# Banded attention of a two-block layer, two heads at a time, with its weights divided ahead of their transposes

## What is computed

```
logits = einsum('bhrnqd,bhrnkd->bhrnqk', qb, kb) * Dh ** -0.5 + bias
p = exp(logits - m); s = sum(p); o = einsum('bhrnqk,bhrnkd->bhrnqd', p, v) / s
A = einsum('bhncd,bhnjd->bhncj', q_in, k_in) * tril
U = einsum('bhnjd,bhnjv->bhndv', k_end, vc)
return intra + inter            # A v + q_in S_prev
```

## Time and profile before

| | |
|---|---|
| median of three runs | 2418.72 us |
| the profiled execution's own time | 2418.39 us |
| its span | 2416.7 us, at a granted clock of 0.998 |
| TensorE busy | 2396.2 us (99%) |
| VectorE, ScalarE, GpSimd busy | 1427.8 (59%), 1189.1 (49%), 216.1 us (9%) |
| moved by DMA | 430.74 MB, mean 178 GB/s |
| chain that ended last | TensorE 97%, VectorE 1%, ScalarE 1% |

### The profile page before, as it was taken

How to read it: one execution, slowest core, us unless ns; L and a number is a source line. 1 busy time by engine, 2 the same in 40 slices (tenths; PEclk the granted TensorE clock), 3 DMA queues, 4 the chain that set the end, 5 groups by cost and what they waited for, 6 DMA issues and landing times.

```text
span 2416.7 us, 28770 instructions
## 1 busy us (share of the span) xinstructions
PE 2396.2 (99%) x11618; PEld 1966.8 (81%) x11618; DVE 1427.8 (59%) x1709; ACT 1189.1 (49%) x1645; POOL 216.1 (9%) x324
## 2 busy tenths in 40 slices
PE   9999999999999999999999999999999999999998
PEld 7888888888888888888887778778888888888886
DVE  5655665565566545665855455567555555556775
ACT  6544554454455445555655344456444444446564
POOL 0052004206200420000000000000000000000000
PEclk9999999999999999999999999999999999999999
DMA  6555455455445555666665444346665555555554
GB/s 207 194 168 162 151 180 175 157 174 157 158 157 174 187 157 179 226 201 200 217 200 185 146 142 140 118 161 202 206 197 184 190 190 191 192 191 192 192 192 139
DMA packets 235970, 430.74 MB, mean 178 GB/s; under 512 B 27492, under 2 KB 30445, under 8 KB 235838
## 3 DMA queue, kind: packets, MB, share of 16 engines
q1 hardware_dynamic: 222848, 413.30, 52.2%
q10 hardware_dynamic: 12990, 15.60, 2.2%
HBM read 423.59 MB, written 5.28 MB: 177 GB/s over the span
## 4 chain that ended last, share of the span: by engine, by line
PE 97%; DVE 1%; ACT 1%; issue 0%; POOL 0%; ACTq 0%; POOLq 0%; DVEq 0%
PE gemm L1323 29%; PE gemm L1325 29%; PE gemm L1324 29%; PE side L889 3%; PE side L1258 1%; PE side L1279 1%; PE side L994 1%; PE side L1244 1%; PE side L899 0%; DVE arena L1744 0%; PE side L1215 0%; PE side L1114 0%; PE side L1060 0%; PE side L998 0%; PE side L962 0%
## 5 line engine op out<-in xcount | busy, mean ns | idle before, releaser
L1738 DVE TENSOR_TENSOR weight_lo<-weight_raw,weight_hi 128x1024 fp32r<-128x1024 f32 x780 | 965.0, 1240 | 762.1 <-ACT weight_hi L1351 761.2
L1351 ACT ACTIVATE weight_hi<-weight_raw 128x1024 fp32r<-128x1024 f32 x780 | 822.1, 1056 | 854.2 <-PE gemm L1325 834.8
L1323 PE MATMUL gemm<-weight_hi,x_hi 128*128 128x512 f32 x2368 | 943.1, 398 | 3.7 <-DVE x_lo L1744 2.1
L1325 PE MATMUL gemm<-weight_hi,x_lo 128*128 128x512 f32 x2368 | 923.5, 390 | 0.0
L1324 PE MATMUL gemm<-weight_lo,x_hi 128*128 128x512 f32 x2368 | 921.9, 389 | 0.0
L1323 PEld LDWEIGHTS gemm<-weight_hi,x_hi 128*128 128x128 f32 x2368 | 444.9, 188 | 102.9 <-issue 12.8
L1325 PEld LDWEIGHTS gemm<-weight_hi,x_lo 128*128 128x128 f32 x2368 | 444.5, 188 | 94.9
L1324 PEld LDWEIGHTS gemm<-weight_lo,x_hi 128*128 128x128 f32 x2368 | 445.2, 188 | 89.4 <-issue 1.4
L1323 PE MATMUL gemm<-weight_hi,lhs_hi 128*128 128x512 f32 x736 | 288.0, 391 | 0.0
L1325 PE MATMUL gemm<-weight_hi,lhs_lo 128*128 128x512 f32 x736 | 287.1, 390 | 0.0
L1324 PE MATMUL gemm<-weight_lo,lhs_hi 128*128 128x512 f32 x736 | 287.1, 390 | 0.0
(11 more groups left out here) (189 smaller groups left out, 1069.3 us busy)
## 6 DMA issues: line engine op xcount, KB each, us to landing
weight_raw<-in_w_in_dram SPq DMA_DIRECT2D x207, 1024.0 KB, 5.1
weight_raw<-in_w_out_dram SPq DMA_DIRECT2D x48, 1024.0 KB, 5.1
weight_raw<-in_w_gate_dram SPq DMA_DIRECT2D x44, 1024.0 KB, 5.1
weight_raw<-in_w_up_dram SPq DMA_DIRECT2D x44, 1024.0 KB, 5.2
weight_raw<-in_w_down_dram SPq DMA_DIRECT2D x44, 1024.0 KB, 5.0
arena<-rel_line ACTq DMA_DIRECT2D x8, 384.0 KB, 5.1
arena<-in_x_dram SPq DMA_DIRECT2D x4, 512.0 KB, 9.3
arena<-delta_blocks ACTq DMA_DIRECT2D x16, 128.0 KB, 5.2
```

Of the source, the lines that this page charges most:

```text
L1323: e.matmul(pair[i][:, :], xh[:, s], wh, start=first, stop=False)
L1325: m = e.matmul(pair[i][:, :], xl[:, s], wh, start=False, stop=last)
L1351: return e.activation(o, i, ACT.Copy, scale=scale)
L1738: return e.tensor_tensor(o, x, y, op)
```

## The change

- The job gv1 stands ahead of av1: gv1 460, av1 468, gr1 476.
- Attention works on pairs of heads (c = 0 to 3 in a half). `alog` of a pair is four matmuls, alternating between the heads, into two banks; VectorE does 4 adds and one maximum over 1024 columns, ScalarE 4 exponentials. `anorm` is new: VectorE takes 4 reciprocals, and GpSimd multiplies the weights (128x1024) by them. `aturn` is 8 transposes into two banks and two copies to a block of its own (`ET`). `apv` has v stationary (128x64) and the turned weights moving (256 columns); the two heads write partitions 0 to 63 and 64 to 127 of a bank that two pairs share. ScalarE copies it, tokens reversed, straight to `acts`. `aout` and `ao` are gone.
- Slots: `alog` 440, 442, 444, 446 (464 to 470), `anorm` three slots behind each, `aturn` five, `apv` 447, 449, 451, 453 in half 0, and 477, 477, 479, 479 in half 1.
- GLA: `gstate` computes both heads in one slot (four matmuls, four banks), every second slot; `go` computes both heads in one slot, and each head has state blocks of its own. `gsq` stands right behind `go`: ScalarE copies the two banks to SBUF and squares from there into PSUM; `ggated` reads SBUF. Slots of hp 0: `gstate` 422, 424, 426, `go` 428, `gsq` 429, the rest as before. Of hp 1: `gsum` 456, 457, `gscore` 459, `gkend` 460, `gstate` 476, 478, 480, `go` 482, `gsq` 483, `ggated` 485, `gout` 486.
- The last VectorE operation of `ggate2` is a step of its own, `ggate3`, three slots later.

```diff
-    j2("aq1", C_AQ + NC), j2("ak1", C_AK + NC), j2("av1", C_AV + NC)
-    j2("gv1", C_GV + NC), j2("gr1", C_GR + NC)
+    j2("aq1", C_AQ + NC), j2("ak1", C_AK + NC)
+    j2("gv1", C_GV + NC), j2("av1", C_AV + NC), j2("gr1", C_GR + NC)
...
+        for c in range(4):
+            put(s + 4 + 2 * c, "alog", half, c), put(s + 7 + 2 * c, "anorm", half, c)
+            put(s + 9 + 2 * c, "aturn", half, c)
+            put(s + 11 + 2 * c if half == 0 else END["av1"] + 1 + 2 * (c // 2), "apv", half, c)
+    gla_at(put, 1, END["aq1"] + 4, END["aq1"] + 7, END["gv1"] + 8, END["gr1"])
...
+def gla_at(put, hp, s, k, v, t):
...
+    for z in range(3):
+        put(v + 2 * z, "gstate", hp, z)
+    put(v + 6, "go", hp), put(v + 7, "gsq", hp)
...
# TensorE
+        def alog(half, c):
...
+            p = [open_bank("alog", half, c, z) for z in range(2)]
             for i in range(NT):
+                for z in range(2):
+                    rows = slice(z * AT_D, (z + 1) * AT_D)
+                    m = e.matmul(p[z][:, i * T:(i + 1) * T], qT[rows, c * T + i * P:c * T + (i + 1) * P],
+                                 kT[rows, c * T:(c + 1) * T], start=True, stop=True)
...
+        def aturn(half, c):
+            E = blk("E", half, c)
+            w.wait_ge(*at("pool:anorm", half, c))
...
+        def apv(half, c):
...
+            p = open_bank("apv", half, c) if c % 2 == 0 else bank("apv", half, c - 1)
+            for k in range(NT):
+                for z in range(2):
+                    at_ = k * NC + (2 * c + z) * AT_D
+                    m = e.matmul(p[z * AT_D:(z + 1) * AT_D, (c % 2) * T:(c % 2 + 1) * T], v[:, at_:at_ + AT_D],
+                                 ET[:, z * NC + k * T:z * NC + (k + 1) * T], start=k == 0, stop=k == NT - 1)
...
+            for hh in range(2):
+                for d, n in ((0, z), (1, NCH - 1 - z)):
+                    b0 = (n % 2) * GL_C
+                    p = open_bank("gstate", hp, z, hh, d)
...
# ScalarE
+            for g in range(2 * NT):
+                s = e.activation(E[:, g * T:(g + 1) * T], E[:, g * T:(g + 1) * T], ACT.Exp, bias=nm[:, g:g + 1],
+                                 accum_out=sums[:, g:g + 1])
...
# VectorE
+            for z in range(2):
+                for i in range(NT):
+                    s = tt(E[:, z * NC + i * T:z * NC + (i + 1) * T], bank("alog", half, c, z)[:, i * T:(i + 1) * T],
+                           Hv[:, (h0 + z) % BANDS, P - i * P:P - i * P + T], ALU.add)
...
+        def anorm(half, c):
+            w.wait_ge(*at("act:alog", half, c))
+            e.reciprocal(stat(2 * NT, "ainv", half, c), stat(2 * NT, "sums", half, c)).then_inc(sem("dve:anorm"))
...
# GpSimd
+        def anorm(half, c):
+            E = by_head(blk("E", half, c))
+            w.wait_ge(*at("dve:anorm", half, c))
+            tt(E, E, over(stat(2 * NT, "ainv", half, c), 2, T), ALU.mult).then_inc(sem("pool:anorm"))
```

More of the change, by code:

```diff
@@ L324, in side_table @@
         put(s + 2 * z, "chan", key, 0), put(s + 2 * z, "chan", key, 2)
-    gla_at(put, 0, s + 4, s + 10, s + 18)
+    gla_at(put, 0, s + 4, s + 8, s + 10, s + 18)
     for half in range(2):
[L327 to L339, removed]
+        s = END[f"ak{half}"]
+        for key, at in ((f"aq{half}", END[f"aq{half}"] + 2), (f"ak{half}", s + 2)):
+            put(at, "chan", key, 0), put(at, "chan", key, 2)
+        for c in range(4):
[3 more added lines that the diff above has]
+    gla_at(put, 1, END["aq1"] + 4, END["aq1"] + 7, END["gv1"] + 8, END["gr1"])
     for n in range(4):
@@ L400 @@
             "dY": ("",), "donorm": ("mean", ""), "mscore": ("w", "den"), "msq": ("mean", ""),
-            "ggate2": ("z", ""), "gsum": ("end", "rest", ""), "gsq": ("mean", ""), "alog": ("b", "")},
+            "gsum": ("end", "rest", ""), "gstate": ("first", ""), "gsq": ("mean", ""), "alog": ("b", "")},
     "pool": {"dinv": ("zero", "")},
@@ L1260, in alog @@
             m.then_inc(sem("pe:alog"))
[L1262 to L1268 removed]
+        def aturn(half, c):
+            E = blk("E", half, c)
+            w.wait_ge(*at("pool:anorm", half, c))
+            for z in range(2):
+                p = open_bank("aturn", half, c, z)
+                for k in range(NT):
+                    for i in range(NT):
+                        at_ = z * NC + i * T + k * P
+                        m = turn(p[:, k * T + i * P:k * T + (i + 1) * P], E[:, at_:at_ + P])
@@ L1635, in gsq @@
             o, ssq = claim("go", hp), stat(2 * NT, "gssq", hp).rearrange("p (h t) -> p h t", t=NT)
-            w.wait_ge(*at("pe:go", hp, 1))
+            w.wait_ge(*at("pe:go", hp))
+            for i in range(NT):
+                s = copy(part(o, i), bank("gpos", hp, i))
+            w.wait_ge(w.own, w.mark(s))
             for i in range(NT):
                 for hh in range(2):
-                    s = e.activation(o[:, (2 * i + hh) * GL_DV:(2 * i + hh + 1) * GL_DV],
-                                     bank("gpos", hp, i)[:, hh * GL_DV:(hh + 1) * GL_DV], ACT.Square,
+                    sl = slice(hh * GL_DV, (hh + 1) * GL_DV)
+                    s = e.activation(bank("gpos", hp, i)[:, sl], part(o, i)[:, sl], ACT.Square,
                                      accum_out=ssq[:, hh, i:i + 1])
@@ L2103, in gscore @@
             p = bank("gscore", hp)
-            Av = [claim("S", hp, d)[:, 3 * GL_DV:BLK].rearrange("p (g c) -> p g c", c=GL_C) for d in range(2)]
+            for hh in range(2):
+                for d in range(2):
+                    claim("S", hp, d, hh)
+            Av = [blk("S", hp, d, 0)[:, 3 * GL_DV:BLK].rearrange("p (g c) -> p g c", c=GL_C) for d in range(2)]
             w.wait_ge(*at("pe:gscore", hp))
```

265 lines of the change are left out of this document (116 added, 149 removed).

## The result

The changed kernel takes **2399.94 us** (median of four runs, 2399.77 to 2402.34) against 2418.76 us (four runs) for the kernel before on the same chip: a ratio of 0.9925, with a 95% interval of 0.9913 to 0.9936. That is 18.8 us less, where 11.7 were forecast. The profiled execution took 2399.88 us, its span is 2398.2 us, 18.5 us shorter than that of before.

The account below looks back on a forecast made before the run. TensorE bounds the kernel: 20.2 us less work, less 8.1 us more waits, clock 0, gives 12.1 us; with 0.4 us off for the gates' score wait, 2418.7 - 11.7 = 2407.0 us. Range 2398 to 2418 us.

Parts of the forecast that it names:

- four waits of 2 us or more that were forecast: Attention transposes: 2.6 us in slots 445 and 469, 4.4 us in 473 for GpSimd's division; 2.1 us in 447 for VectorE's adds.
- The wait for VectorE in 486: Last linear-attention transposes: the wait of 3.6 us shrinks to 1.5 us, because squares and power move into slot 483.
- TensorE's work: TensorE's queue: 20.2 us less, 18.0 us from two attention halves and 2.2 us from grouped states and outputs.
- The 0.2 us credited to the outputs: Linear attention: two outputs in one slot save a switch of form, counted as 0.2 us in all.
- price of 0.53 us for an overlapping pair: Logit, value and state matmuls: two in different array halves overlap when alternating, and cost 0.53 us together.
- Waits and clock: TensorE's waits: new 14.3 us against old 6.2, so +8.1 us; clock falls net 0, bounds -2.7 to +8.1 us.
- the walk through the queues: Attention stage: engine queues followed from slot 440's start; one loop takes some 9.8 us per two slots, TensorE needs 7.8.
- a longer wait in the gates' score: Linear attention's gates: the score, now two slots behind its sum instead of four, waits longer; 0.4 us charged.
- A: Attention loop keeps up: only the 1.5 us wait stays, 27.6 us less, 2391 us; chance 0.14.
- B: Gain is eaten: exponentials cost 0.69 us, waits near 20 us, clock falls twice more, 2418 us; chance 0.19.
- D: Slower: every loop price at its upper end, waits 24 us, clock falls behind each long wait, 2424 us; chance 0.07.
- C: Matmul pairs do not overlap: 32 pairs cost 17 us more but cover most new waits, 2415 us; chance 0.08.

Follow-up runs that it names:

- first two experiments: Changed kernel with a pair's matmuls issued head by head instead of alternating: in the logits 2401.23 us, in the values 2402.61 us.
- values serial: Changed kernel with a pair's value matmuls issued head by head instead of alternating, without a wait between heads: 2402.61 us.
- later transposes: Changed kernel with the last transposes of linear attention one slot later (487 instead of 486): 2400.36 us.
- late squares: Changed kernel with the squares of the last two linear-attention heads back at slot 484, behind the last gate's tanh: 2407.12 us.
- logits serial: Changed kernel with a pair's logit matmuls issued head by head instead of alternating, without a wait between heads: 2401.23 us.
- the spread kernel with the division on VectorE: Changed kernel with attention pairs three slots apart, division one slot behind the logits and on VectorE, last linear-attention transposes one slot later: 2391.03 us.
- both drained kernels: Changed kernel, head by head, TensorE waiting for the first head's matmuls to end before the second's: logits 2403.56 us, values 2408.52 us.
- drained logits: Changed kernel with logits head by head, TensorE waiting for the first head's matmuls to end before the second's: 2403.56 us.
- the kernel before with later transposes: Kernel before the change, with only its last linear-attention transposes one slot later (487 instead of 486): 2414.92 us (ten runs).

## Why the forecast was right, and where its size was off

**Direction and mechanism** were right. TensorE bounds the kernel, its queue became shorter, and a part of that came back as waits of the transposes for the new division. Of the four waits of 2 us or more that were forecast, those in slots 445, 469 and 473 came; the one in 447 did not. The wait for VectorE in 486 came too (1.71 us at full clock, forecast 1.5).

**TensorE's work** fell by about 2.4 us more than forecast, term by term: logit pairs 1.29 instead of 1.40 us (eight: 0.9 us), values and eight transposes 2.09 instead of 2.2 us (eight: 0.9 us), state slots 1.28 instead of 1.40 us (six: 0.7 us). Each time I had put the way in and out at 0.34 us from a slot with one overlapping pair; a step with two pairs pays less for it. The 0.2 us credited to the outputs did not come: two in one slot take 6.36 us (1555.36 to 1561.72), twice the 3.18 of before. The forecast's price of 0.53 us for an overlapping pair is the right one; the alternation of the matmuls, which it gave as the reason, is not needed for it (first two experiments).

**Waits and clock** were over-counted, and here lies the step that failed. It was not the walk through the queues. Counted from the start of slot 440 (1391.26 us), the walk had TensorE at slot 445's transposes at 17.7 us and the multiply done at 20.3; measured are 17.5 and 20.5 (1408.94 + 2.79). It had the fourth pair's adds done at 31.4 us; measured is 31.35. GpSimd's and VectorE's side of it, in the kernel after:

```profile
1408.94 2.79 POOL L2279 TENSOR_TENSOR arena<-arena,stats 128x1024 f32<-128x1024 f32 x1 [49.95 <-DVE stats L2177]
1418.30 1.90 POOL L2279 TENSOR_TENSOR arena<-arena,stats 128x1024 f32<-128x1024 f32 x1 [6.58 <-DVE stats L2177]
```
```profile
1408.77 1.20 DVE L1749 TENSOR_TENSOR weight_lo<-weight_raw,weight_hi 128x1024 fp32r<-128x1024 f32 x1
...
1410.55 1.41 DVE L1749 TENSOR_TENSOR arena<-side,arena 128x256 f32<-128x256 f32 x4
...
1416.91 1.22 DVE L1749 TENSOR_TENSOR weight_lo<-weight_raw,weight_hi 128x1024 fp32r<-128x1024 f32 x1 [3.50 <-ACT weight_hi L1351]
...
1418.82 2.46 DVE L1749 TENSOR_TENSOR weight_lo<-weight_raw,weight_hi 128x1024 fp32r<-128x1024 f32 x1 [0.60 <-ACT weight_hi L1351]
1421.21 1.40 DVE L1749 TENSOR_TENSOR arena<-side,arena 128x256 f32<-128x256 f32 x4
```

The loop's length stands in these rows too: the adds of pairs 2 and 3 begin 10.66 us apart (1410.55 and 1421.21), where TensorE needs 7.53 us for two slots. Pair 3's logits were no reason: TensorE began them at 1418.32 us and needs 1.13 us for them.

The exclusion works in both orders: the multiply that starts behind a split takes 2.79 us, and the split that starts behind a multiply takes 2.46 us instead of 1.22. The Trainium skill (SBUF — State Buffer, Who interferes with whom) says that a VectorE instruction with two SBUF inputs contends with a GpSimd instruction that reads SBUF, and that the order of issue decides who blocks. The trace agrees, with these numbers.

What failed is how waits and clock were put together:

- *Half 0.* Forecast: waits of 2.6, 2.1 and 0.4 us at full clock. Measured: one wait of 2.98 us, then a fall that cost 2.8 us, and no wait in 447 and 449. TensorE came to slot 447's transposes at 1423.36 us, 32.1 us after the start instead of 29.4; the adds were done. The slow clock spent the time that would have been waited. Three other profiled executions show the trade: where the first fall was shorter and cost some 1.5 us (values serial, later transposes, late squares), the transposes of slot 449 wait 0.69 to 0.71 us; where it was as long as here (logits serial), they do not wait. Sum: 5.1 forecast, 5.8 measured.
- *Half 1.* Forecast: 2.6, 0.7 and 4.4 us, and a fall of 2.7 us behind the last. Measured: 2.17 and 2.54 us, with a fall of 1.6 us behind the first and none behind the last. Sum: 10.4 forecast, 6.3 measured. TensorE stood at slot 473's transposes when forecast (35.5 us after the start of 464, against 35.2), but pair 2 was divided after 38.0 us instead of 39.5. Half 1 has no band to load, so ScalarE issues no DMA ahead of its exponentials; VectorE idles about 3.1 us for ScalarE there and 3.50 us in half 0. I had walked half 0 and priced half 1 with it.

Together: 2.4 us of work, 4.1 us of waits and clock in half 1, less 0.7 us in half 0 and 0.2 us in slot 486, 0.4 us for a longer wait in the gates' score, which was forecast and did not come, and 0.8 us that are not the change's (the start and the shorter waits outside the stage): 6.8 us, the difference between 11.7 and the 18.5 of the profiled execution. No row of the trace stood behind the 0.4 us. The errors in the work and in half 1 point the same way, so the forecast was too careful, not lucky.

**The rivals.** *A* (the loop keeps up, 2391 us) is near what the spread kernel with the division on VectorE made of it, with more room and another engine, though 3.4 us of waits are left there where A had 1.5. *B* and *D* priced waits and falls as a sum; slots 447 and 449 show that one takes the place of the other, at least in part. *C* (no overlap) is refuted by the rows and by both drained kernels. The rule that the forecast set beside C, that weight loads overlap a running matmul only if the row group differs (the Trainium skill, TensorE: Matmul & The Clock Gate, The mechanism), does not price this form: the value pairs share all 128 rows, and four of their matmuls take 1.08 us, against 2.21 us drained.

**Not settled.** When the clock falls (below). The grouped states and outputs and the move of gv1 had no experiment of their own; what they brought is read from the rows. And runs of the changed kernel lie up to 2.6 us apart (2399.77 and 2402.34 us). A further fall of the clock is not the reason: the slowest of the four has the highest granted clock (0.998 against 0.997). The start may be a part of it, but only one execution of each kernel was profiled.

## What to carry to other kernels

When TensorE's side work shrinks, walk the whole loop that feeds it (here adds, maximum, exponentials, splits, division): once TensorE was faster than this loop, moving a step or giving it to another engine only renamed the wait, and a wider spacing removed the waits of the transposes. Within such a stretch waits and clock falls were not to be added up, for a fall used time that would have been waited. Before small differences are explained by the edit, look at whether the traces already differ ahead of it: here up to 1.7 us did. And an edit that brings nothing in a full loop (the division on VectorE) can bring 3 us once the loop has room, so it is worth trying again then.

## What the hardware showed that was not expected

- Matmuls in two halves of the array overlap also when they are issued as runs, one half's two first: 1.14 us for four logit matmuls in either order and 2.31 us when drained; 1.08, 1.09 and 2.21 us for the values, whose halves are columns and not rows.
- A wait's length alone does not decide the clock. In the fourteen profiled executions it fell behind all waits of 2.9 us or more and behind those of 2.16, 2.49, 2.53 and 2.56 us; it did not fall behind 2.35, 2.40, 2.46 and 2.54 us. Behind 2.17 us it fell in two kernels (the changed one and that with the later transposes) and not in a third (late squares). Shorter waits mostly left it alone, but not always: it fell 2 us behind one of 1.29 us in the kernel before with later transposes, and behind the 1.56 us ahead of the first product in four of the fourteen.
- A fall could come late: behind the wait of 2.93 us in the kernel with drained logits the transposes still ran at full speed (1.09 us for eight), and the granted clock was 0.72 in the stretch from 1524 to 1530 us behind them.
- The price of a fall was not fixed: about 2.8 us for the first one of the changed kernel and about 1.5 us for that of the kernel with serial values, in the same slot and behind waits of 2.98 and 2.99 us.
